# A decoder block in float32r: the input projection as seven products of halves, and the first tap of each convolution on ScalarE

## The reference, cut to what matters

```python
xn = rmsnorm(h, norm_w)                        # h: 16 meta tokens + 512 tokens, 2048 wide
proj = xn @ w_in                               # w_in: 2048 x (2*1024 + 4*2048 + 2*16 + 2*2048)
u_pool, z_pool, q, k, v, z_dn, b, a, gate_pool, gate_dn = jnp.split(proj, splits, axis=-1)
y_pool = causal_multiscale_pool(u_pool, pool_mix, pool_scale) * silu(z_pool)
y_dn = gated_deltanet_branch(q, k, v, z_dn, b, a, conv_w, A_log, dt_bias, dn_norm_w)
merged = sigmoid(gate_pool) * (y_pool @ w_pool_out) + sigmoid(gate_dn) * (y_dn @ w_dn_out)
return h + merged @ w_o
```

## Time and profile before

| | before |
|---|---|
| time, median of 3 runs (lowest to highest) | 1962.79 us (1962.67 to 1963.48) |
| the profiled execution: span, first to last instruction | 1960.8 us |
| the profiled execution's own time | not stated apart; the median is 2.0 us over its span |
| TensorE busy | 1931.4 us (99%) |
| VectorE busy | 921.4 us (47%) |
| ScalarE busy | 726.0 us (37%) |
| GpSimd busy | 78.3 us (4%) |

### The profile page before, as it was taken

One profiled execution on the slowest core, in us unless ns is written; L12 is line 12 of the kernel. 1 busy time (PEld: TensorE's weight loads), 2 busy tenths in 40 slices (PEclk: granted clock), 3 DMA queues, 4 the chain that ended last, 5 costly groups with the idle time before them and its releaser, 6 DMA issues.

```text
span 1960.8 us, 35753 instructions
## 1 busy us (share of the span) xinstructions
PE 1931.4 (99%) x13729; PEld 1724.3 (88%) x13729; DVE 921.4 (47%) x2315; ACT 726.0 (37%) x2136; POOL 78.3 (4%) x105
## 2 busy tenths in 40 slices
PE   5999999999999999999999999999999999999998
PEld 5888899999999999999999988888888888888886
DVE  6333343656556466555646654322224444335332
ACT  5422223435353443535345353323234322224232
POOL 4000000000000000000000000000000000000000
PEclk8999999999999999999999999999999999999999
DMA  6133342433333242333334144333443534347302
GB/s 222 59 103 102 102 134 88 119 95 86 95 120 90 87 124 69 96 111 100 91 107 123 44 131 127 119 107 128 134 162 134 186 118 139 118 139 279 108 22 86
DMA packets 221302, 225.73 MB, mean 115 GB/s; under 512 B 33665, under 2 KB 197978, under 8 KB 220522
## 3 DMA queue, kind: packets, MB, share of 16 engines
q1 hardware_dynamic: 158898, 180.17, 28.1%
q10 hardware_dynamic: 55944, 22.63, 4.6%
q0 software_dynamic: 6336, 21.08, 3.4%
HBM read 199.65 MB, written 25.30 MB: 115 GB/s over the span
## 4 chain that ended last, share of the span: by engine, by line
PE 97%; ACT 1%; DVE 1%; issue 0%; POOL 0%; DMA 0%; ACTq 0%; SPq 0%; DVEq 0%
PE pj L530 82%; PE pg L530 10%; PE pt L530 3%; PE pt L679 1%; PE pg L781 0%; POOL xl L1696 0%; DVE fst L1233 0%; ACT xsquare L908 0%; DMA xt<-in_meta_tokens 0%; PE pj L574 0%; DVE xl L1239 0%; ACT wh L868 0%; DVE xt L1246 0%; ACT L1041 0%; ACT L1070 0%
## 5 line engine op out<-in xcount | busy, mean ns | idle before, releaser
L530 PE MATMUL pj<-xh,wh 128*128 128x512 f32 (+3 forms) x2688 | 735.1, 328 | 3.2 <-DVE wl L1208 3.1
L530 PE MATMUL pj<-xh,wl 128*128 128x512 f32 (+3 forms) x2688 | 712.4, 319 | 0.0
L530 PE MATMUL pj<-xl,wh 128*128 128x512 f32 (+3 forms) x2688 | 712.3, 319 | 0.0
L1208 DVE TENSOR_TENSOR wl<-raw,wh 128x256 fp32r<-128x256 f32 x896 | 344.2, 421 | 603.0 <-ACT wh L868 601.5
L530 PEld LDWEIGHTS pj<-xh,wh 128*128 128x128 f32 x2688 | 446.9, 189 | 43.2 <-DVE wl L1208 3.4
L530 PEld LDWEIGHTS pj<-xh,wl 128*128 128x128 f32 x2688 | 448.4, 188 | 35.9
L530 PEld LDWEIGHTS pj<-xl,wh 128*128 128x128 f32 x2688 | 448.8, 189 | 33.9 <-issue 1.0
L868 ACT ACTIVATE wh<-raw 128x256 fp32r<-128x256 f32 x896 | 307.0, 410 | 64.7 <-issue 45.0
L868 ACT ACTIVATE wh<-rawb 128x256 fp32r<-128x256 f32 (+1 forms) x224 | 85.0, 437 | 217.0 <-PE pj L530 189.8
L530 PE MATMUL pj<-yl,wh 128*128 128x512 f32 x384 | 149.5, 389 | 0.0
L530 PE MATMUL pj<-yh,wl 128*128 128x512 f32 x384 | 149.5, 389 | 0.0
(11 more groups left out here) (243 smaller groups left out, 1784.3 us busy)
## 6 DMA issues: line engine op xcount, KB each, us to landing
raw<-in_w_in SPq DMA_DIRECT2D x112, 1024.0 KB, 6.2
rawb<-in_w_dn_out SPq DMA_DIRECT2D x16, 1024.0 KB, 6.3
rawb<-in_w_o SPq DMA_DIRECT2D x12, 1024.0 KB, 5.3
gates_scratch<-stg ACTq DMA_DIRECT2D x32, 256.0 KB, 2.1
rawb<-in_w_pool_out SPq DMA_DIRECT2D x8, 1024.0 KB, 5.7
gst<-gates_scratch POOLq DMA_DIRECT2D x32, 256.0 KB, 3.1
yraw<-branch_scratch SPq DMA_DIRECT2D x1, 5632.0 KB, 23.1
xt<-in_x SPq DMA_DIRECT2D x4, 1024.0 KB, 6.2
```

The source lines that it names most:

```text
L530: return pe.matmul(dst, lhs, rhs, start=start, stop=stop)
L1208: tt(wl[:, j, 2 * q:2 * q + 2, :], raw[:, 2 * par + h, 2 * q:2 * q + 2, c * P:(c + 1) * P], wh[:, j, 2 * q:2 * q + 2, :].bitcast(F32), ALU ...
```

## The change

Activations are cut into 2 x 2 quarters (half of the k-tiles by half of the tokens, 264 tokens with 8 of the meta tokens), the 256 columns of a weight block also into 2 x 2 (half of the k-tiles by 128 columns). A block is then a 2 x 2 product of halves, made with seven products instead of eight. It takes four sums of weight quarters per block on VectorE (`s1` to `s4`), four sums of activation quarters once at the start (`x_sums`), and sums of PSUM results at the end of a block (`c11`, `c21`, `c22`). `ORDER` gives the products; `NEXT` is product 7 of the following block. Each product is two chunks of four k-tiles by three terms: 12 matmuls. A block has 14 chunks, 168 matmuls; the first has 16 and the last 12.

ScalarE makes `wh` in pieces of 128 x 512, three chunks ahead (`AHEAD`), and copies three half results per block out of PSUM (`snap`). VectorE makes `wl` in pieces of the same size (L1493). Raw weights come as four quarters of 512 KB with rows of 512 bytes. Finished heads go through `head_d` in HBM (stored by ScalarE, loaded again by SP). There are 28 hooks in a block, and step m of a pair stands at hook 15m//8. The first tap of each head is a ScalarE copy with a scale (`first_tap`); taps 1 to 3 stay on VectorE (L1801). On GpSimd `tm` now shares its memory with `zst`, and the loads of the next pair's rows wait until the store has landed.

```diff
+NEXT = 0
+ORDER_FIRST = (1, 2, 7, 6, 4, 5, NEXT, 3)
+ORDER = (1, 4, 6, 2, 5, NEXT, 3)
+ORDER_LAST = (1, 4, 6, 2, 5, 3)
+AHEAD = 3
+RINGS = 4
...
-        lay.skip_to(WORK)
-        raw = lay.tensor("raw", [4, UK, CW])
-        xh = lay.tensor("xh", [KT, TP], F32R)
...
-        wh = lay.tensor("wh", [4, UK, P], F32R)
-        wl = lay.tensor("wl", [4, UK, P], F32R)
...
+        xh, xl = {}, {}
+        for product_of in XPLACE:
+            xh[product_of] = lay.tensor(f"xh{product_of}", [KH, TH], F32R)
+            xl[product_of] = lay.tensor(f"xl{product_of}", [KH, TH], F32R)
...
+        raw = lay.tensor("raw", [5, KH, P])
+        wh = lay.tensor("wh", [RINGS, HK, P], F32R)
+        wl = lay.tensor("wl", [RINGS, HK, P], F32R)
+        snap = lay.tensor("snap", [3, TH])
...
+            def block_loads(b, col, between=None):
+                order, base = order_of(b), base_of(b)
+                sp.wait_ge(lo_done, base + after(order, 1))
+                load_raw(RA, col)
+                sp.wait_ge(sum_done, 4 * b + 3)
+                load_raw(RC, col)
+                if between == "v":
+                    load_vch(between_pair[0])
+                sp.wait_ge(lo_done, base + after(order, 5))
+                load_raw(RF, col)
+                if between == "kq":
+                    load_kq(between_pair[0])
+                if between == "z":
+                    load_zst(between_pair[0])
+                sp.wait_ge(lo_done, base + after(order, 3))
+                load_raw(RB, col)
...
+        def delta_step(h):
+            return next((m for m in range(O0 + 6) if 15 * m // 8 == h), None)
...
+        def split_target(b, par, t):
+            order, at = order_of(b), t + AHEAD
+            if at >= 2 * len(order):
+                at, b, par = at - 2 * len(order), b + 1, 1 - par
+                order = order_of(b)
+            start = 0 if isinstance(b, int) and b == 0 else 2 * par + 2
+            return b, order[at // 2], at % 2, base_of(b) + at, (start + at) % RINGS
...
-                if not early:
-                    pe.wait_ge(lo_done, 16 * cp + 8 * c + 4 * h + 4)
-                if h == 0:
-                    need(pe, proj_evac, 2 * cp + c - 1)
...
-                    for w, xx, first, last in ((wh, xh, True, False), (wh, xl, False, False), (wl, xh, False, True)):
-                        for dst, c0, n in halves:
-                            mm = product(dst, w[:, slot, k, :], xx[:, kt, c0:c0 + n],
-                                         first and kt == 0, last and kt == KT - 1)
...
+            def block_products(b, par, kind, kind_next, hook):
+                order, base = order_of(b), base_of(b)
...
+                for i, what in enumerate(order):
+                    if what == 1:
+                        need(pe, last_done, b - 1)
+                    elif what == 2:
+                        need(pe, add_done, 3 * b)
...
+                    elif what == 3:
+                        pe.wait_ge(add_done, added(b, "C22"))
+                    elif what == NEXT:
+                        pe.wait_ge(add_done, added(b, "C21"))
+                    c0 = c0_of(kind_next if what == NEXT else kind)
+                    bank = bank_a[par] if what in (1, 6, 5, 3) else bank_c if what == 2 else bank_b
+                    opens, closes = what in (1, 2, 7, NEXT), what in (3, 2, 4)
...
+                        pe.wait_ge(lo_done, base + chunk + 1)
+                        for k in range(HK):
+                            kt = HK * h + k
+                            for w, xx, one, last in ((wh, xh, True, False), (wh, xl, False, False), (wl, xh, False, True)):
+                                mm = pe.matmul(bank[:, c0:TH], w[:, slot, k, :], xx[what][:, kt, c0:TH],
+                                               start=opens and one and kt == 0, stop=closes and last and kt == KH - 1,
+                                               skip_group_check=True)
...
+                of, what, half, chunk, slot = split_target(b, par, t)
+                need(act, pe_chunk, chunk - RINGS + 1)
...
+                        act.wait_ge(sum_done, summed(of, {6: "S2", 5: "S1", 3: "S4"}[what]) if what != NEXT else summed(of + 1, "S3"))
+                copy(wh[:, slot, :, :], raw[:, SLOT_OF[what], HK * half:HK * (half + 1), :]).then_inc(hi_done, 1)
+            def block_acts(b, par, kind, kind_next, event, hook):
+                order, base = order_of(b), base_of(b)
+                for t in range(2 * len(order)):
+                    split_hi(b, par, t)
+                    c0 = c0_of(kind)
...
+            def first_tap(p, k, c):
...
+                else:
+                    act.wait_ge(last_done, b + 1)
+                need(act, head_stored[c], 16 * (4 * p + k))
+                w = convcur[:, 3, (1, 0, 2)[k], c:c + 1]
+                act.activation(stg[:, c, :], xin[:, 3:3 + T], ACT.Copy, scale=w).then_inc(conv_step, 1)
...
+            def split_lo(b, par, t):
...
+                of, what, half, chunk, slot = split_target(b, par, t)
+                dve.wait_ge(hi_done, chunk + 1)
+                tt(wl[:, slot, :, :], raw[:, SLOT_OF[what], HK * half:HK * (half + 1), :], wh[:, slot, :, :].bitcast(F32),
+                   ALU.subtract).then_inc(lo_done, 1)
...
+            def s2(b):
...
+                tt(raw[:, RE, :, :], raw[:, RE, :, :], raw[:, RF, :, :], ALU.add).then_inc(sum_done, 1)
...
+                dve.wait_ge(lo_done, base_of(b) + after(order_of(b), 4))
+                tt(raw[:, RF, :, :], raw[:, RC, :, :], raw[:, RF, :, :], ALU.add).then_inc(sum_done, 1)
...
+            def c21(b, kind, dst):
+                order = order_of(b)
+                dve.wait_ge(snap_done, snapped(b, "s2"))
+                dve.wait_ge(pe_chunk, base_of(b) + max(after(order, 4), after(order, 6)))
+                for part, cols in placed(kind, 0, dst):
+                    ins = tt(part, bank_b[:, cols], snap[:, 1, cols], ALU.subtract)
+                ins.then_inc(add_done, 1)
...
+                for t in range(2 * len(order)):
+                    if t == (3 if first else 0):
+                        s2(b)
...
+                    if not last and t == (9 if first else 6):
+                        s3(b + 1)
+                    split_lo(b, par, t)
+                    if t == (10 if first else 7):
+                        free(1)
+                        c21(b, kind, dst[1])
+                    if t == (12 if first else 10):
+                        c22(b, par, kind, dst[1])
...
+                    if t == (13 if kind in ("k", "q", "v") or first else 12 if kind == "u" else 11):
+                        free(0)
+                        c11(b, kind, dst[0])
...
-                if tap == 0:
...
-                    need(dve, *((tok_done, p * ALL_TOK - SLOTS) if k == 2 else (silu_done, p * 3 - 1)))
-                    dve.wait_ge(conv_cur, p + 1)
-                    dve.tensor_scalar(acc, xin[:, src_tap:src_tap + T], w, None, ALU.mult).then_inc(conv_step, 1)
-                else:
-                    dve.wait_ge(conv_step, n + tap)
-                    dve.scalar_tensor_tensor(acc, xin[:, src_tap:src_tap + T], w, acc, ALU.mult, ALU.add).then_inc(conv_step, 1)
+                dve.wait_ge(conv_step, n + tap)
+                dve.scalar_tensor_tensor(acc, xin[:, src_tap:src_tap + T], w, acc, ALU.mult, ALU.add).then_inc(conv_step, 1)
...
-            with pool.Fori(0, PAIRS) as d:
+            def row_differences(d):
...
+            def head_out(d):
                 pool.wait_ge(y_ready, 2 * d + 2)
-                pool.dma_start(y_d[bass.ds(PW + CW * d, CW), :].rearrange("(h e) t -> e h t", e=P), zst[:, :, :]).then_inc(y_stored, 16)
...
+            row_differences(0)
+            with pool.Fori(1, PAIRS) as d:
+                head_out(d - 1)
+                pool.wait_ge(y_stored, 16 * d)
+                row_differences(d)
+            head_out(PAIRS - 1)
```

More of the change, by code:

```diff
@@ L74, with base_of, order_of, after @@
 NGATE = 2 * D // CW
-CB = 512
-NCB = D // CB
 NCP = CP_GATE0 + NGATE
+SLOT_OF = {1: 0, 2: 1, 3: 1, 4: 3, 5: 3, 6: 4, 7: 4, NEXT: 4}
+RA, RB, RC, RF, RE = range(5)
+def base_of(b):
+    return 0 if isinstance(b, int) and b == 0 else 14 * b + 2
+ALL_CHUNKS = base_of(NCP - 1) + 2 * len(ORDER_LAST)
+def order_of(b):
+    if isinstance(b, int):
+        return ORDER_FIRST if b == 0 else ORDER_LAST if b == NCP - 1 else ORDER
+    return ORDER
+def after(order, product):
+    return 2 * order.index(product) + 2
 CI = 0
@@ new lines, in free, with hook @@
+                    def free(c, k=k):
+                        if k == 3:
+                            dve.wait_ge(head_stored[c], 16 * (4 * p + 3))
+                        else:
+                            need(dve, conv_step, (6 * p + 2 * k + 1 - c) * 4)
+                    def hook(h, k=k):
+                        m = delta_step(28 * k + h)
+                        if d is not None and m is not None:
+                            delta(d, m)
```

(14 more changed lines are left out.)

1025 lines of the change are left out of this document (645 added, 380 removed).

## The result

The changed kernel takes 2074.34 us (median of 4 runs, 2063.57 to 2078.57), before 1962.75. The ratio is 1.0558, 95% interval 1.0531 to 1.0585: **5.6% slower**, where 1930 us were forecast. The profiled execution took 2078.57 us, its span 2077.0.

What follows compares the result with a forecast made beforehand. TensorE's own stream bounds the kernel, busy for 1931.4 of 1960.8 us. 1960.8 - 128.4 saved + 95.5 of losses = 1927.9 for the span, plus 2.0 for the median: 1930 us; its own range 1903 to 1957, the whole range 1884 to 1972.

Steps and rivals of the forecast that it cites:

- What the change gives TensorE: All blocks: 168 products a block instead of the rows before, 20.5, 20.2 or 19.9 us a block, 128.4 us saved.
- What it asks of VectorE: Pair loop: 14.2 us a block against 5.4 before, VectorE busy for 97 of 105.5 us in a pair.
- three bursts: Pairs: stalls priced at 5 us for the inverse, 2.5 for the decays and 2 for ScalarE's issues of DMAs.
- The clock: Rival, pairs: the longest stall drops TensorE's clock, 1.5 us a drop, one or two in each pair; 1945 us, chance .06.
- The inverse: In q of each pair: VectorE's row of work takes 15.0 us, TensorE is there after 10.3; 5 us lost a pair.
- ScalarE's own share: Pairs: three DMA issues for the inverse block ScalarE for 4.8 us, with two pieces against 4.4 of cover; 2 us a pair.
- The decays: Start of a pair: the store's landing (4.2 us) precedes the loads, `dec` comes 5 us into it; 2.5 us for six pairs.
- First taps at no cost: Pairs: six first taps of .6 us on ScalarE lie beside TensorE at no cost, at most 3.6 us a pair without cover.
- The end: The start of branch products: 2 us lost.
- The head: Before and in block 0: VectorE's 32.7 us of work delays TensorE by 6 us (3 to 12).
- The loads of raw weights: Gates: DMA share could be .8, still under one; the rival that loads are late by 1 us a block: 1986, chance .04.
- The rival with too short a lead: Pair loop: every burst becomes a stall, slower above 13.2 us a pair; 1989 us at 17 a pair, chance .16.

Runs made afterwards that it cites:

- e11_no_sums: The changed kernel with the four sums of weight quarters cut to 8 columns of one k-tile in all blocks but the first (wrong weights): 1991.95 us.
- e3_stalls: The changed kernel with artificial waits of TensorE of about 0.5 to 8 us in gate blocks; no total given, a block with 4.60 us idle grew by 6.93.

## Why the prediction was wrong

In short: the prediction failed in two steps. It put the fall of the clock at nothing in its sum, where the runs show some 91 us. And it put the waits at 95.5 us, where 148.6 were measured, having taken VectorE at 92% of a pair as bearable and having no term for the turn of the loop.

- **What the change gives TensorE: right.** Gate blocks take 19.88 us (forecast 19.9), u and v without DeltaNet 20.25 (20.5), and q's products go 120 ns apart, which makes 20.2. Before, they took 21.8, 23.4 and 22.4, so the gain is 28 x 1.9 + 20 x 3.2 + 8 x 2.1 = 134 us, for 128.4 forecast.
- **What it asks of VectorE: right in amount, wrong in use.** 697.58 / 7 = 99.7 us a pair, forecast 97. The forecast took 92% as bearable and priced three bursts; e11_no_sums, without the four sums, is 82 us faster, at least 50 of them beyond what the clock varies by.
- **The clock: the step that failed most.** It was a rival with 1.5 us a fall, one or two in each pair, chance .06. A single fall costs 2.1 to 2.3 us (e3_stalls), so that price was near. But the forecast's own wait of 4.7 us in each pair was as long as the one that took the clock down in e3_stalls, so falls belonged in the main sum, and in v blocks one costs 9 to 10 us. Together some 91 us.
- **The inverse: right place, other chain.** 4.12 us of wait in q for 5 forecast, but through ScalarE's queue: sum, piece, SiLU, squares, transposes. The forecast had no DeltaNet products of TensorE in that stretch, and four of those, the transposes, were what waited. It had put ScalarE's own share on the loads of the inverse.
- **The decays: mis-sized and hidden.** The store took 8.3 us to land (7.54 waited and .74 to issue), not 4.2. The DMA engines are full in both stretches (share 1.01, before 1.06), but between issue and landing they move some 2.6 MB instead of 1.4: three quarters of weights, 1 MB of k and q and two stores of heads stand beside it, and the forecast had taken over the landing of the kernel before. So `dec` was there 6.2 us into the pair (forecast 5). Behind the loop's turn it cost little, without that turn 6.65 us a pair. The forecast's own sum also has a slip: 5 + 1.2 + 1.14 + .6 is 7.9 and not 8.4, so its terms give 2.0 and not 2.5 us.
- **The turn of the loop: missing.** 4.1 us in each of six pairs. Under a lead of 11.7 us nothing of it showed.
- **First taps at no cost: wrong, by little.** Their place in ScalarE's queue, ahead of pieces of wh, lengthened the wait in q by 1 us in each pair, 7 in all. Before the change it costs 5 us as well.
- **The end: mis-sized.** 2 us forecast, 17.3 us idle and 5.5 of clock measured. ScalarE meets the load of 5 MB with pieces of weights behind it.
- **The head:** 6 and 4 and 3 forecast with pooling, 16.1 idle and 11 of clock measured, the same kind.
- **The loads of raw weights** were hidden, as forecast: no wait of TensorE's names them.
- **The rival with too short a lead** came nearest. It had the mechanism (stalls of a pair above 13.2 us), with 14.4 of idle time and 9 of clock measured in each; its price, 17 at .16, and the range's end at 1972 were too low.

What stays open: why a v block of the same instructions falls to half clock in one pair and not in another, and how much of each wait is the sums' own, since removing either the sums or the other causes gains more than its share. No run lengthens the lead itself: it is three chunks in all of them, so that a longer lead would have saved the change is argued and not shown.

## What to carry to other kernels

A cut in the bounding engine's work is worth its size only while its feeders keep their lead. Before trading TensorE's products for VectorE's sums, list every place where a feeder stands still for longer than the new lead, the turns of loops and queued DMAs among them, and price each stall of more than a few microseconds with the clock's fall besides. Where the clock falls in some executions and not in others, compare idle times before times. Then spread the feeders' work: the same DeltaNet over five blocks instead of four gained 22 us.

## What was not expected of the hardware

ScalarE and VectorE stood for 5.5 and 5.2 us at each turn of a long loop, waiting for nothing that the profile shows; written out, the loop has no such gap. In the gate blocks a wait of TensorE of up to 2.37 us left the clock at full, one of 4.60 us took it to half for 6.8 us at a cost of 2.3, and one of 9.05 us cost no more. In the pairs the same instructions had 82 to 133 us at half clock, which is up to 25 us of time.
